# A weight ring of 22 slots in place of 19, in space taken from the descriptor reserve

## What is computed

```python
NE, CAP, FF = 16, 64, 2048                     # experts, tokens of each, hidden width
def expert_choice_ffn(h, w_router, w_gate, w_up, w_down):
    aff = softmax(h @ w_router)                # 512 tokens x 16 experts
    g, idx = top_k(aff.T, CAP)
    xe = h[idx]                                # per expert 64 x 1024
    hid = silu(xe @ w_gate) * (xe @ w_up)      # 64 x 2048
    ye = (hid @ w_down) * g                    # 64 x 1024
    return zeros_like(h).at[idx].add(ye)
out = rms_norm(x + expert_choice_ffn(rms_norm(x, g2), ...), gf)
```

## Time and profile before

| | us |
|---|---|
| Median of 3 runs | 2046.56 (2043.48 to 2046.97) |
| Profiled execution, its own time | 2046.65 |
| Span of the profile, first to last instruction | 2044.8 |

### The profile page before, as it was taken

How to read it: one execution, slowest core, us unless ns; L and a number is a source line. 1 busy time by engine, 2 the same in 40 slices (tenths; PEclk the granted TensorE clock), 3 DMA queues, 4 the chain that set the end, 5 groups by cost and what they waited for, 6 DMA issues and landing times.

```text
span 2044.8 us, 20714 instructions
## 1 busy us (share of the span) xinstructions
PE 1918.6 (94%) x8778; PEld 1154.6 (56%) x8778; DVE 716.7 (35%) x1131; ACT 520.2 (25%) x811; POOL 68.7 (3%) x58
## 2 busy tenths in 40 slices
PE   7999999999999999999996999988898988888998
PEld 6787788888888787876873333333233333232332
DVE  6544444333356665776454111101111110111111
ACT  5443432322245343267532000000000000000001
POOL 2000000000014001100020000000000000000000
PEclk9999999999999999999998999999999999999999
DMA  4221142332322223111373999999999999999996
GB/s 168 91 93 52 52 143 94 95 102 93 112 95 103 83 102 126 52 63 52 104 316 148 419 428 427 428 427 428 426 428 427 428 427 428 426 428 427 427 428 290
DMA packets 59004, 505.36 MB, mean 247 GB/s; under 512 B 7504, under 2 KB 8016, under 8 KB 31264
## 3 DMA queue, kind: packets, MB, share of 16 engines
q1 hardware_dynamic: 58592, 503.87, 61.2%
q10 hardware_dynamic: 320, 0.17, 0.0%
HBM read 499.82 MB, written 4.19 MB: 246 GB/s over the span
## 4 chain that ended last, share of the span: by engine, by line
PE 61%; DMA 24%; issue 6%; DVE 3%; ACT 3%; POOL 1%; ACTq 0%; DVEq 0%; POOLq 0%
PE ps L1895 32%; DMA ring_a<-in_experts_in 16%; DMA ring_b<-in_experts_in 8%; PE ps L2240 8%; PE ps L2229 8%; PE ps L1852 4%; PE ps L2190 3%; PE ps L2249 1%; PE ps L1946 1%; PE ps L1943 1%; DVE d_lo L1155 1%; POOL xacc L701 1%; PE ps L2212 1%; POOL gbl L735 0%; ACT hidT L1125 0%
## 5 line engine op out<-in xcount | busy, mean ns | idle before, releaser
L2229 PE MATMUL ps<-ring_a,xe 128*64 128x512 f32 x1408 | 317.7, 599 | 42.9 <-DMA ring_a<-in_experts_in 42.0
L1155 DVE TENSOR_TENSOR d_lo<-d_raw,d_hi 128x1024 fp32r<-128x1024 f32 x168 | 209.0, 1253 | 124.9 <-ACT d_hi L756 124.5
L2229 PEld LDWEIGHTS ps<-ring_a,xe 128*64 128x64 f32 x1408 | 97.6, 137 | 258.0 <-issue 189.6
L1364 DVE TENSOR_TENSOR hid<-hid,ps 128x512 f32<-128x512 f32 x32 | 20.6, 684 | 458.8 <-PE ps L2229 458.8
L1895 PE MATMUL ps<-n_hi,d_hi 128*128 128x512 f32 x448 | 175.6, 392 | 1.5 <-DVE d_lo L1155 0.8
L756 ACT ACTIVATE d_hi<-d_raw 128x1024 fp32r<-128x1024 f32 x168 | 172.9, 1049 | 8.9 <-DMA d_raw<-in_tiles_in 8.2
L1895 PE MATMUL ps<-n_hi,d_lo 128*128 128x512 f32 x448 | 174.4, 389 | 0.0
L1895 PE MATMUL ps<-n_lo,d_hi 128*128 128x512 f32 x448 | 174.3, 389 | 0.0
L2229 PE MATMUL ps<-ring_b,xe 128*64 128x512 f32 x640 | 148.1, 608 | 26.4 <-DMA ring_b<-in_experts_in 26.4
L2240 PE MATMUL ps<-ring_a,hidT 128*64 128x512 f32 x704 | 157.1, 595 | 4.6 <-ACT hidT L1125 3.9
L1775 DVE TENSOR_TENSOR x<-x,ps 128x1024 f32<-128x1024 f32 x60 | 69.2, 1215 | 259.7 <-PE ps L2212 259.7
(11 more groups left out here) (433 smaller groups left out, 2701.3 us busy)
## 6 DMA issues: line engine op xcount, KB each, us to landing
ring_a<-in_experts_in SPq DMA_DIRECT2D x114, 2048.0 KB, 40.8
ring_b<-in_experts_in SPq DMA_DIRECT2D x57, 2048.0 KB, 41.0
d_raw<-in_tiles_in SPq DMA_DIRECT2D x168, 512.0 KB, 3.4
ring_a<-in_experts_in SPq DMA_DIRECT2D x36, 1024.0 KB, 34.6
ring_b<-in_experts_in SPq DMA_DIRECT2D x6, 1024.0 KB, 9.9
x_in<-in_xT_in SPq DMA_DIRECT2D x4, 512.0 KB, 6.4
x<-in_xT_in SPq DMA_DIRECT2D x1, 2048.0 KB, 8.0
x_store<-x SPq DMA_DIRECT2D x1, 2048.0 KB, 9.9
```

Source lines behind the costliest of these rows:

```text
L1155: dve.tensor_tensor(d_lo[:, n % SLOTS, :, :], d_raw[:, n % SLOTS, :, :], d_hi[:, n % SLOTS, :, :].bitcast(F32), ALU.subtract).then_inc(t_l ...
L1364: return dve.tensor_tensor(out, a, b, ALU.mult)
L2229: mm = pe.matmul(ps[half * CAP:(half + 1) * CAP, 2 * m + q, :], xe[:, k, :], slot(e, n)[:, (2 * q + half) * S:(2 * q + half + 1) * S], sta ...
```

## The change

The ring gets 22 slots. `ring_a` grows to 16 slots, `ring_b` keeps 6. The kernel asks for a descriptor reserve of 128 bytes in place of the default, which moves its base down; places from 192 KiB up are moved up by 16 KiB, so that `ring_a` can reach from 80 to 208 KiB. The expert stage's small buffers leave 80 to 88 KiB and share places above 192 KiB with one another (`hid` with `hidT`, `ye` with `xg`, `place` with `pickg` and the routing buffer `awc`); `gbc`, `zsq` and `fin` of the final norm move to the region of `ring_b`. `LATE` = 2 is the number of slots that lie under `xT`. `ring_moves` now never meets an odd boundary: behind the first 24 single chunks every DMA carries a pair up to the last four.

```diff
-RING, RING_A, RING_B = 19, 12, 6
+RING, RING_A, RING_B = 22, 14, 6
+LATE = RING - RING_A - RING_B
+SCRATCH = 128
@@ ring_moves
-        n = 1 if g < RING + 2 or g >= end - 4 or g % RING in (RING_A - 1, RING - 2) else 2
+        n = 1 if g < RING + 2 or g >= end - 4 or g % RING in (RING_A - 1, RING_A + RING_B - 1) else 2
@@ at
+            kb += 16 if kb >= 192 else 0
@@ buffers
-        ring_a = at("ring_a", [P, RING_A + 1, FF], 88)
+        ring_a = at("ring_a", [P, RING_A + LATE, FF], 80)
...
-        hid = at("hid", [P, 2, S], 80)
-        hidT = at("hidT", [P, 2, 4, P], 84)
-        ye = at("ye", [P, S], 201.5)
-        place = at("place", [P, S], 203.5)
-        zsq = at("zsq", [P, D], 80)
-        gbc = at("gbc", [P, D], 144)
-        fin = at("fin", [P, TT, D], 152)
+        hid = at("hid", [P, 2, S], 201.5)
+        hidT = at("hidT", [P, 2, 4, P], 201.5)
+        ye = at("ye", [P, S], 199.5)
+        place = at("place", [P, S], 197.5)
+        zsq = at("zsq", [P, D], 4)
+        gbc = at("gbc", [P, D], 0)
+        fin = at("fin", [P, TT, D], 16)
@@ slots
-            if RING_A <= s < RING - 1:
+            if RING_A <= s < RING - LATE:
                 rows = ring_b[:, s - RING_A:s - RING_A + n, :]
             else:
-                s = (s + 1) % RING
+                s = (s + LATE) % RING
@@ sync queue
             load_weights(5, RING_A)
             stage_done(sp, "out2", 7)
-            load_weights(RING_A, RING - 1)
+            load_weights(RING_A, RING - LATE)
             sp.wait_ge(t_pe.sem, t_pe.count("x3"))
-            load_weights(RING - 1, len(MOVES))
+            load_weights(RING - LATE, len(MOVES))
@@ kernel
-    nc = bacc.Bacc("TRN2", target_bir_lowering=False, num_devices=1)
+    nc = bacc.Bacc("TRN2", target_bir_lowering=False, num_devices=1, dynamic_dma_scratch_size=SCRATCH)
```

More of the change, by code:

```diff
@@ L303, in kernel_program @@
         x1 = at("x1", [P, KD, S], 176)
-        R = at("R", [P, S], 204.75)
+        R = at("R", [P, S], 204.6875)
         junk = at("junk", [P, GH, GDV], 124)
@@ L381, in kernel_program @@
         iot = at("iot", [P, CAP], 207.25)
-        top8 = at("top8", [NE, 8], 207.5)
+        top8 = at("top8", [NE, 8], 193.875)
         aw = at("aw", [NE, S], 202.5)
-        awm = at("awm", [NE, S], 80)
-        awc = at("awc", [NE, S], 82)
+        awm = at("awm", [NE, S], 194.5)
+        awc = at("awc", [NE, S], 196.5)
         xe = at("xe", [P, KD, CAP], 194.5)
-        xg = at("xg", [P, S], 196.5)
-        pick = at("pick", [P, TT, CAP], 198.5)
-        pickg = at("pickg", [P, TT, 2, CAP], 199.5)
-        hid = at("hid", [P, 2, S], 80)
-        hidT = at("hidT", [P, 2, 4, P], 84)
-        ye = at("ye", [P, S], 201.5)
-        place = at("place", [P, S], 203.5)
-        zsq = at("zsq", [P, D], 80)
-        gbc = at("gbc", [P, D], 144)
-        fin = at("fin", [P, TT, D], 152)
+        xg = at("xg", [P, S], 199.5)
+        pick = at("pick", [P, TT, CAP], 196.5)
+        pickg = at("pickg", [P, TT, 2, CAP], 197.5)
+        hid = at("hid", [P, 2, S], 201.5)
[5 more added lines that the diff above has]
+        fin = at("fin", [P, TT, D], 16)
         ident = at("ident", [P, P], 192)
@@ L404, in kernel_program @@
         dsm = at("dsm", [P, 64], 194.25)
-        m01 = at("m01", [P, 2, P], 206.75)
+        m01 = at("m01", [P, 2, P], 206.6875)
         scr = [at(f"scr{n}", [P, S + 4], 194.5 + 2.03125 * n) for n in range(5)]
```

## The result

The changed kernel takes 2032.49 us (median of 4 runs, 2031.15 to 2034.3) against 2046.76 us (4 runs). The ratio is 0.9933, 95% interval 0.9921 to 0.9945: 14 us less, where 7.4 were forecast.

What follows compares the result with a forecast made beforehand. Bound: the expert stage's full DMA stream, with PE waiting, then a fixed tail. Three chunks' lead gave 7.4 us, all else 0: 2044.8 - 7.4 = 2037.4, plus 1.85 outside the span, 2039.2 us; range 2035.5 to 2043.

Steps and rivals of the forecast that it cites:

- The holes as cover for the three chunks: Idle DMA ahead of the expert stage, 1076 to 1088 and 1108 to 1121 us, hides the extra chunks' loading.
- The first load into a used slot: Start of the full stream: still issued at 1123.59 us, when PE has finished chunk 0, now carrying chunk 22, not 19.
- The price of the lead: Expert-stage stream: three chunks more ahead, at 2.467 us each, make later chunks land 7.40 us earlier.
- The last wait ahead of chunk 368: Last expert: PE's last wait for a transfer stays ahead of chunk 368, ending at about 1985 us, before at 1992.32.
- the tail: PE's work after the last wait for a transfer, from 1992.32 us: nothing becomes late, so it costs what it did.
- PE's waits for the ring: Sign in the changed profile: PE's waits for ring chunks down by 7 us, from 69 to about 62.
- What they bring: Part on three chunks more in the expert-stage stream: every later chunk lands 7.40 us earlier.
- The step on the reserve: Smaller descriptor reserve: it serves software descriptors, and every load of the rows runs on the sync queue; cost 0.
- The sign that the prediction gave for the stream: Expert-stage transfers after about 1123.6 us should run at 425 to 428 GB/s; 423 or less would prove the prediction wrong.
- The ten DMAs less: Rival: moves after the first fill fall from 194 to 184, gaining 3.3 us on top, 2035.9 us; chance 0.04.
- The deeper queue: Rival: three more chunks in flight lower the landing rate; at 2.50 us per chunk 2051.1 us, slower; chance 0.03.
- The two views that decided against them: Full-stream rates: single chunks and pairs both move 427 GB/s; no slice of 20 us is below 424 GB/s.

Runs made afterwards that it cites:

- the ladder from 19 to 22 slots on the grain: Small reserve, buffers starting on multiples of 256 bytes: kernel before with 19 slots, changed kernel with 20, 21, 22: 2039.3, 2037.5, 2035.8, 2032.5 us.

## Why the prediction was wrong

**What held.** What bounds the kernel: the DMA stream from 1124 us on, with PE waiting for it; the end as one landing plus a fixed tail. The holes as cover for the three chunks. The first load into a used slot at the same moment (1123.49). The price of the lead: 7.4 us forecast; 6.8 by the ladder from 19 to 22 slots on the grain (7.6 by the ratios), 6.1 for the same three chunks off it (2046.3 - 2040.23), and 5.2 us for two chunks off it (2045.93 - 2040.68), where 4.9 were expected. (The 7.4 in the split of the trace is three times the old price of a chunk, and no test of it.) The last wait ahead of chunk 368, and the tail, to 0.1 us. PE's waits for the ring fell from 69 us to 61.7 (44.8 + 16.9 in the page's groups), where about 62 was forecast:

```profile
L2232 PE MATMUL ps<-ring_a,xe 128*64 128x512 f32 x1472 | 330.8, 596 | 45.8 <-DMA ring_a<-in_experts_in 44.8
L2232 PE MATMUL ps<-ring_b,xe 128*64 128x512 f32 x576 | 129.7, 596 | 17.0 <-DMA ring_b<-in_experts_in 16.9
```

(Groups of the changed kernel's page: count, busy us, mean ns of one, idle us before them and its releaser.) That number came out right by luck: the last landing moved by 13.1 us, so the waits should have shrunk by more. The rest is in PE's work. From 1124 us to the last wait's end, before and after, and one short stretch of before:

```profile
1124.00:1992.32 868.32, 793.08 (x3655) 277.98 (x3651) 123.80 (x164) 53.39 (x93) 0.00 (x0) 0.99 1.01 427
1124.00:1979.22 855.22, 787.31 (x3655) 278.63 (x3651) 123.87 (x164) 53.30 (x93) 0.00 (x0) 1.00 1.01 429
1582.90:1586.30 3.40, 3.40 (x10) 0.97 (x8) 0.00 (x0) 0.00 (x0) 0.00 (x0) 0.51 1.02 434
```

The same 3655 instructions keep PE busy 5.8 us less (787.31 against 793.08). Before, the granted clock is at its lower level (0.50 to 0.51, 1.2 GHz) for 3.4 us three times in this part, from 1582.9, 1770.7 and 1879.9 us; each time PE has just ended a wait of 2.0 to 2.6 us. In the changed kernel's profile there is no such stretch between 1119 and 2030 us. Where PE waits for the stream afterwards, that slower work costs nothing, but it fills time that would be waiting, and so a sum of waits is no measure of the shift. The shared buffers brought no wait: behind 1979.5 us PE waits only for the same three hand-overs as before, 0.7 to 0.8 us each.

**The step that failed** is in "What they bring": "From there the stream has no idle time to lose or gain, so every later chunk lands 3 x 2.467 = 7.40 us earlier". The stream was full, but full isn't a fixed rate. I carried 2.467 us per chunk over to a kernel in which every destination address had moved. The step on the reserve put its cost at 0 because the loads run on the sync queue, and never priced the move of the base that comes with it; of the other engines the section on the change says "nothing changes but addresses", and addresses were taken for nothing. What the runs showed in its place: on a multiple of 256 a chunk costs 2.459 us in place of 2.475. With 348 chunks on the path, those 0.016 us are 5.6 us, three quarters of the term that was worked out with care. The sign that the prediction gave for the stream, 425 to 428 GB/s, was missed on the upper side (431), and the last wait ended at 1979.2 us, not 1985.

**The rivals.** The ten DMAs less were priced at up to 3.3 us: nothing that shows (the run with 32 more single chunks). By the packets a single chunk does hold an engine longer: 8 x 309 ns against 4 x 611, 28 ns more, or 0.9 us for those 32. (The 2.0 us per DMA that stands beside this rival is, in the Trainium skill, "DMA: Bandwidth & Descriptors", section "Anatomy of one DMA", a fit for DMAs issued from GpSimd; the loads here are issued by the sync queue.) The deeper queue was to lower the rate: 427 GB/s at 21 and 22 slots off the grain, so neither lower nor higher. The two views that decided against them (rates of singles and of pairs; slices of 20 us) could not show the true cause, because the whole ring of the kernel before stands at one alignment. The Trainium skill, "SBUF — State Buffer", section "Operand start alignment", says of starts at an element's size that the rule "is about legality, not speed"; nothing in this kernel broke it, and the runs here show that a ring 32, 64 or 128 bytes off 256 is legal and costs about 0.3% of the kernel.

## What to carry to other kernels

Where a stage runs at the rate of its transfers, multiply before you call a small thing free: the price of one transfer times their number is the stage, and whatever touches all of them (destination address, row length, cut) needs a bound of its own, even when the diff shows it only as a changed base. Put the destination of bulk loads on a multiple of 256 bytes; here moving the old kernel by 128 bytes, with no other edit of weight, brought 6.5 us, nearly as much as three more slots in the ring. Lead in a ring is worth what it was reckoned at: one chunk's time per slot, as long as idle transfer time ahead of the stage covers the loading.

## What the runs showed of the hardware

A full stream of loads from HBM into rows of 16 KiB per partition, with some of 8 KiB, moves 430 to 431 GB/s with all destinations on a multiple of 256 bytes, and 427 with all of them 32, 64 or 128 bytes over one; 512 is no better than 256. The cost is 3.7 to 4.8 ns per packet in the mean, with 8 KiB as with 16 KiB, and six slots of 19 off the grain, all in a row, cost nothing that shows.

The sync queue holds its issues once about ten such DMAs are outstanding, that is, issued and not landed. In the traces of 19 to 22 slots every issue between 1140 and 1900 us with up to eight outstanding took at most 0.62 us, nearly all of them 0.328; with ten outstanding the median is 3.5 to 4.2 us. So issue takes 0.328 us in the median with 19 or 20 slots, where a lap of the ring is ten DMAs; with 22 slots and eleven DMAs it is 1.6 us, and with the same slots cut into twelve DMAs a lap it is more. The lines of the loads with 20 slots, and with 22 slots and twelve DMAs (issue ns, smallest, median and largest, 1140 to 1900 us):

```profile
L639 SPq DMA_DIRECT2D ring_a<-in_experts_in x113: 327/328/2222, 1141.3 to 1896.8; - x113
```

```profile
L639 SPq DMA_DIRECT2D ring_a<-in_experts_in x132: 327/2226/11315, 1141.1 to 1897.3; - x132
L639 SPq DMA_DIRECT2D ring_b<-in_experts_in x45: 327/4202/11550, 1146.2 to 1882.2; - x45
```

It cost nothing here (the run with twelve DMAs took 2030.74 us), and each held DMA of that run had the work of nine or more others ahead of it. What it would cost a queue that also carries something urgent wasn't tried.
